# Decoder layer on one core: queries turned one tile further ahead in two attention stages, compression rows turned first, four stores issued one stage later

## What is computed

```python
def compress_kv(rows, cmp_pe, cmp_w1, cmp_b1, cmp_w2, k_norm_cmp):
    ...                                  # blocks of 32 rows, stride 16, flattened
    h = jax.nn.gelu(jnp.einsum('bngcf,cfh->bngch', flat, cmp_w1) + cmp_b1)
    out = jnp.einsum('bngch,chd->bngcd', h, cmp_w2)
    return rmsnorm(out[..., 0, :], k_norm_cmp), out[..., 1, :], end_pos

k_c, v_c, end_c = compress_kv(kv_cmp_p, cmp_pe, cmp_w1, cmp_b1, cmp_w2, k_norm_cmp)
o_cmp_p, p_cmp_p = dense_attend(q_p, k_c, v_c, end_c[None, :] <= pos_p[:, None])
...
def mem_attend(q_raw, kv_mem, mem_q_norm):
    q = rmsnorm(q_raw.reshape(B, S, MEM_H, 1, MEM_HD), mem_q_norm)
    o, _ = dense_attend(q, kv_mem[..., 0, :], kv_mem[..., 1, :], ...)
```

## Time and profile before

| | us |
|---|---|
| median of the timed runs | 2593.41 |
| the profiled execution, its own time | 2588.36 |
| its span, first to last instruction | 2586.8 |
| last copy of the projection ends, to first matmul of the memory stage | 656.49 to 660.17 |
| memory stage, first matmul to last copy | 660.17 to 721.59 |
| turning stage | 721.92 to 754.90 |
| compressed attention | 755.23 to 794.99 |

### The profile page before, as it was taken

How to read it: one execution, slowest core, us unless ns; L and a number is a source line. 1 busy time by engine, 2 the same in 40 slices (tenths; PEclk the granted TensorE clock), 3 DMA queues, 4 the chain that set the end, 5 groups by cost and what they waited for, 6 DMA issues and landing times. The chain is left out here.

```text
span 2586.8 us, 40413 instructions
## 1 busy us (share of the span) xinstructions
PE 2395.7 (93%) x15386; PEld 2183.8 (84%) x15386; DVE 1212.6 (47%) x2152; ACT 817.1 (32%) x1787; POOL 318.3 (12%) x568
## 2 busy tenths in 40 slices
PE   6998897999767999878899999999999999999999
PEld 6977787999666889844499999987999999999997
DVE  4457665314647867556532323333443333333334
ACT  5354463444335665423231212121311111111110
POOL 1004221011103422265200000000000000000000
PEclk9988699999988999989999999999999999999999
DMA  4012432321110000077311112130211111111111
GB/s 150 24 34 65 135 113 82 93 102 30 43 35 1 1 1 2 18 189 185 97 50 38 48 50 82 49 115 1 82 49 33 49 50 49 49 33 50 50 33 66
DMA packets 216764, 156.77 MB, mean 61 GB/s; under 512 B 76722, under 2 KB 197733, under 8 KB 216516
## 3 DMA queue, kind: packets, MB, share of 16 engines
q1 hardware_dynamic: 187124, 122.06, 16.6%
q0 software_dynamic: 8096, 18.98, 2.7%
q10 hardware_dynamic: 21360, 13.22, 1.8%
HBM read 142.76 MB, written 15.59 MB: 61 GB/s over the span
## 5 line engine op out<-in xcount | busy, mean ns | idle before, releaser
L177 PE MATMUL ps<-brT_r,ff_wih 128*128 128x344 f32 x1008 | 322.0, 319 | 0.0
L179 PE MATMUL ps<-brT_r,ff_wi_r 128*128 128x344 f32 x1008 | 321.6, 319 | 0.0
L178 PE MATMUL ps<-xnT_r,ff_wih 128*128 128x344 f32 x1008 | 321.3, 319 | 0.0
L3749 ACT ACTIVATE ff_sa<-ps 128x344 f32<-128x344 f32 x66 | 30.3, 459 | 563.4 <-PE ps L179 563.3
L177 PE MATMUL ps<-x_r,mg_wh 128*128 128x344 f32 x576 | 185.4, 322 | 6.8 <-DVE xnT_r L165 6.8
L177 PEld LDWEIGHTS ps<-brT_r,ff_wih 128*128 128x128 f32 x1008 | 189.6, 188 | 1.0
L179 PEld LDWEIGHTS ps<-brT_r,ff_wi_r 128*128 128x128 f32 x1008 | 189.4, 188 | 0.0
L178 PEld LDWEIGHTS ps<-xnT_r,ff_wih 128*128 128x128 f32 x1008 | 189.0, 187 | 0.4
L178 PE MATMUL ps<-xnT_r,mg_wh 128*128 128x344 f32 x576 | 184.7, 321 | 0.0
L3785 DVE TENSOR_TENSOR x<-x,ps 128x512 f32<-128x512 f32 (+1 forms) x198 | 134.8, 685 | 101.0 <-PE ps L179 100.2
L179 PE MATMUL ps<-x_r,mg_w_r 128*128 128x344 f32 x552 | 176.2, 319 | 0.0
(11 more groups left out here) (615 smaller groups left out, 5879.6 us busy)
## 6 DMA issues: line engine op xcount, KB each, us to landing
ff_wi<-in_w_ffn_in SPq DMA_DIRECT2D x42, 512.0 KB, 5.2
mg_w<-in_w_in SPq DMA_DIRECT2D x23, 512.0 KB, 4.1
ff_wo<-in_w_ffn_out SPq DMA_DIRECT2D x11, 1024.0 KB, 4.9
s_pages<-in_cache_kv_slc POOLq DMA_DIRECT2D x128, 64.0 KB, 2.9
s_pages<-in_cache_kv_slc SPq DMA_DIRECT2D x128, 64.0 KB, 2.8
sc_X<-in_cache_kv_cmp SPq DMA_DIRECT2D x56, 128.0 KB
sc_X<-in_cache_kv_cmp POOLq DMA_DIRECT2D x56, 128.0 KB, 2.4
mg_w<-in_w_branch SPq DMA_DIRECT2D x23, 256.0 KB, 4.5
```

What stands on the lines that cost most here:

```text
L177: nc.tensor.matmul(out, wh, xh, start=(first and k == 0), stop=False)
L178: nc.tensor.matmul(out, wh, xl, start=False, stop=False)
L179: ins = nc.tensor.matmul(out, wl, xh, start=False, stop=(last and k == n - 1))
L3749: nc.scalar.activation(sa[:, s % 2, :], ps[:, s % 2, 0:BLK], ACT.Silu).then_inc(silued, 1)
```

## The change

- In both attention stages, round i now begins with turn(i+3) on PE and with keep_q(i+3) on ACT. Before, these stood behind turn_p(i+1) and keep_p(i+1). The start is reordered to match.
- In the turning stage the x items come first. ACT copies two of them and DVE two. PE waits for w1 alone ahead of the hidden layer. w2 and gcmp are loaded from POOL's queue. Both memsets stand at the start of DVE's stream, and the copies of vc2 stand behind the sum of squares.
- The four stores of the projection stage are issued in the memory stage, behind kv_mem_prompt.

```diff
@@ stage_tok_proj, SP
                 sp.wait_ge(kept, xlast[KV] + 1)
-                sp.dma_start(O["kv_slc_prompt"]..., kvsw[:, 0:QT, 0:256]).then_inc(out, 16)
-                sp.dma_start(O["kv_slc_sample"]..., kvsw[0:B, QT, 0:256]).then_inc(out, 16)
-                sp.dma_start(O["win_prompt"]..., kvsw[:, QT - 4:QT, 256:512]).then_inc(out, 16)
-                sp.dma_start(O["win_sample"][:, WIN - 1]..., kvsw[0:B, QT, 256:512]).then_inc(out, 16)
                 sp.wait_ge(moved, 16)
@@ stage_turn
-        for r in range(4): ... items.append(("k", r, half))
-        for g in range(G): ... items.append(("x", g, half))
+        items = [("x", g, half) for g in range(G) for half in range(2)]
+        NX = len(items)
+        items += [("k", r, half) for r in range(4) for half in range(2)]
@@ stage_turn, SP and POOL
-                sp.dma_start(w2[:, :, :], I["cmp_w2"].rearrange("c h d -> h c d")).then_inc(in_w, 16)
-                sp.dma_start(gcmp[:, :], I["k_norm_cmp"].partition_broadcast(P)).then_inc(in_w, 16)
+                pool.dma_start(w2[:, :, :], I["cmp_w2"].rearrange("c h d -> h c d")).then_inc(in_w2, 16)
+                pool.dma_start(gcmp[:, :], I["k_norm_cmp"].partition_broadcast(P)).then_inc(in_w2, 16)
@@ stage_turn, PE
-                    if n >= 4:
-                        pe.wait_ge(kept, n - 3)
-                        pe.wait_ge(klow, min(n - 3, 8))
+                    if n >= 2 * NX:
+                        pe.wait_ge(klow, n - 2 * NX + 1)
+                    elif n >= NX:
+                        pe.wait_ge(kept_a if n % 2 == 0 else kept_v, (n - NX) // 2 + 1)
...
-                pe.wait_ge(in_w, 64)
-                pe.wait_ge(kept, len(items))
+                pe.wait_ge(in_w, 32)
+                pe.wait_ge(kept_a, NX // 2)
+                pe.wait_ge(kept_v, NX // 2)
...
-                pe.wait_ge(hready, 1)
+                pe.wait_ge(in_w2, 32)
+                pe.wait_ge(klow, 8)
                 pe.wait_ge(activated, 2)
@@ stage_turn, ACT and DVE
+                    elif n % 2 == 0:                     # ACT: x items 0 and 2
+                        for dst, rows in rows_x(n): nc.scalar.activation(dst, rows, ACT.Copy)
+                        if n % 2:                        # DVE: x items 1 and 3
+                            for dst, rows in rows_x(n): nc.vector.tensor_copy(dst, rows)
@@ stage_turn, DVE
+                nc.vector.memset(vc2[:, :, :], 0.0).then_inc(hready, 1)
+                nc.vector.memset(kc2[:, :, :], 0.0).then_inc(hready, 1)
...
-                dve.wait_ge(activated, 2)
-                nc.vector.memset(vc2[:, :, :], 0.0).then_inc(hready, 1)
                 dve.wait_ge(outp, 1)
-                for k in range(2):
-                    nc.vector.tensor_copy(vc2[k * 64:k * 64 + NC, ...], o4[:, 1])
                 ... # ko, its square, the sum, kmean
+                for k in range(2):
+                    nc.vector.tensor_copy(vc2[k * 64:k * 64 + NC, ...], o4[:, 1])
                 dve.wait_ge(kroot, 1)
-                chain.link(dve, nc.vector.memset(kc2[:, :, :], 0.0))
@@ stage_cmp_prompt and stage_mem_prompt, PE (ACT likewise with keep_q, exponentials, keep_p)
                 for i in range(QT):
+                    if i + 3 < QT:
+                        turn(i + 3)
                     if i + 2 < QT:
                         scores(i + 2)
                     if i + 1 < QT:
                         turn_p(i + 1)
-                    if i + 3 < QT:
-                        turn(i + 3)
                     attend(i)
@@ stage_mem_prompt, SP
                 sp.dma_start(O["kv_mem_prompt"]..., kvm[:, :, :]).then_inc(A["prep_out"], 16)
+                ... # the four stores, in the same order
```

More of the change, by code:

```diff
@@ L1582, in stage_turn, with rows_x @@
         klow = sem("klow")
[L1584 to L1590, removed]
+        items = [("x", g, half) for g in range(G) for half in range(2)]
+        NX = len(items)
+        items += [("k", r, half) for r in range(4) for half in range(2)]
+        def rows_x(n):
+            _, r, half = items[n]
+            for cc in range(2):
+                for par in range(2):
+                    yield (xc[par * HD:(par + 1) * HD, cc, r, half * 256:(half + 1) * 256],
+                           ps[cc * HD:(cc + 1) * HD, n % 4, :].rearrange("p (t e) -> p t e", e=2)[:, :, par])
         with st.block() as block:
@@ L1638, in _ @@
                 for n, (kind, r, half) in enumerate(items):
-                    act.wait_ge(turned, n + 1)
                     if kind == "k":
[L1641 to L1649, removed]
+                        act.wait_ge(turned, n + 1)
+                        high(nc, kT[0:HD, r, half * 512:(half + 1) * 512], ps[0:HD, n % 4, :]).then_inc(khigh, 1)
+                    elif n % 2 == 0:
+                        act.wait_ge(turned, n + 1)
+                        for dst, rows in rows_x(n):
+                            ins = nc.scalar.activation(dst, rows, ACT.Copy)
+                        ins.then_inc(kept_a, 1)
                 act.wait_ge(hid, 1)
@@ L1662, in _ @@
             def _(dve):
-                for n, (kind, r, half) in enumerate(items[:8]):
+                nc.vector.memset(vc2[:, :, :], 0.0).then_inc(hready, 1)
+                nc.vector.memset(kc2[:, :, :], 0.0).then_inc(hready, 1)
+                for n, (kind, r, half) in enumerate(items):
+                    if kind == "x":
+                        if n % 2:
+                            dve.wait_ge(turned, n + 1)
+                            for dst, rows in rows_x(n):
+                                ins = nc.vector.tensor_copy(dst, rows)
+                            ins.then_inc(kept_v, 1)
+                        continue
                     cols = slice(half * 512, (half + 1) * 512)
-                    dve.wait_ge(kept, n + 1)
+                    dve.wait_ge(khigh, n - NX + 1)
                     low(nc, kT[HD:P, r, cols], ps[0:HD, n % 4, :], kT[0:HD, r, cols]).then_inc(klow, 1)
-                dve.wait_ge(in_w, 64)
-                dve.wait_ge(activated, 2)
-                nc.vector.memset(vc2[:, :, :], 0.0).then_inc(hready, 1)
-                dve.wait_ge(hready, 1)
+                dve.wait_ge(hready, 2)
+                dve.wait_ge(in_w2, 32)
                 dve.wait_ge(outp, 1)
                 o4 = ps[0:NC, 0, 0:4 * HD].rearrange("p (c g d) -> p c g d", c=2, g=2)
-                for k in range(2):
-                    nc.vector.tensor_copy(vc2[k * 64:k * 64 + NC, :, k * HD:(k + 1) * HD], o4[:, 1])
                 chain.link(dve, nc.vector.tensor_copy(ko[:, :, :], o4[:, 0]))
@@ L1803, in _ @@
                         keep_p(i + 1)
-                    if i + 3 < QT:
-                        keep_q(i + 3)
             @block.vector
@@ L2261, in _ @@
                 exponentials(0)
+                keep_q(2)
                 exponentials(1)
-                keep_q(2)
                 keep_p(0)
                 for i in range(QT):
+                    if i + 3 < QT:
+                        keep_q(i + 3)
                     if i + 2 < QT:
```

28 lines of the change are left out of this document (16 added, 12 removed).

## The result

The changed kernel took 2578.35 us (median of 4 runs, 2569.68 to 2579.30), beside it the kernel before 2594.03 (4 runs, 2590.64 to 2599.18): ratio 0.9928, 95% interval 0.9904 to 0.9952. Between the medians it is 15.7 us less. On another chip it gave 2576.96 against 2589.32 (5 and 16 runs): ratio 0.9948, 0.9930 to 0.9965, or 12.4 us less between the medians. The prediction was 2577.5, a gain of 15.9, which lies inside both intervals.

What follows compares the result with a forecast made beforehand. It took stage barriers and, in both attention stages, a ring through the query copy keep_q as bounds, no engine. Gains of 3.1 + 4.7 + 2.4 + 5.7 = 15.9 us from 2593.41 gave 2577.5, range 2571 to 2585.5.

Steps and rivals of the forecast that it cites:

- Stores: Barrier between projection and memory stage: without SP's four stores there, PE starts 3.15 us earlier; taken as 3.1.
- the cover on SP: Memory stage: SP's moved issues end 3.6 us before its next one, which waits for POOL, so they delay nobody.
- Memory stage: Rounds fall from 6.45 to 5.41 us once scores no longer wait for keep_q; five rounds 5.2, net 4.7.
- The head: Start of the memory stage: turn(3) now stands before scores(2) on PE, costing 0.57 us.
- Turning stage: Hidden layer starts 1.35 us earlier, memset of vc2 off the chain 0.43, vc2 copies 0.58; sum 2.4.
- the move of w2 and gcmp to POOL's queue: Turning stage: these 96 KB beside w1 delay it by 0.4 us at w1's rate, of which 0.3 was taken.
- The other two terms: Turning stage behind the hidden layer: no wait for the vc2 memset, 0.43 us; vc2 copies inside DVE's wait, 0.58.
- Compressed attention: Same ring through keep_q opened: rounds fall from 4.59 to 3.61 us, the head costs 0.2; net 5.7.
- Sum: All four parts together, 3.1 + 4.7 + 2.4 + 5.7 = 15.9 us, giving 2577.5; chance 0.68.
- The rival of more than the sum: PE's bound in the memory stage and a warm hidden layer give 2 to 3 us more, 2574.5; chance 0.05.
- DVE's ring: Memory stage: maximum to end of scaling 4.78 us plus output copy 0.63 bounds the new round at 5.41.
- The rival on the other side, the clock: Later stages: 50 us more at TensorE's 1.2 GHz level make the kernel slower, 2602.5 us; chance 0.04.

Runs made afterwards that it cites:

- e3: Changed kernel with w2 and gcmp loaded from SP's queue behind w1, not from POOL's: 2578.52 us, ratio 0.9966 to the kernel before.
- e5: Changed kernel with POOL issuing the w2 and gcmp loads only once w1 has landed: 2579.94 us, ratio 0.9964 to the kernel before.
- e9: Changed kernel run again unaltered, beside the kernel before on another chip: 2576.96 us, ratio 0.9948.
- e2: Changed kernel with the four stores issued at the end of the projection stage again: 2585.84 us, ratio 0.9982 to the kernel before.
- e10: Changed kernel with w2 and gcmp loaded once w1 has landed and POOL's rotation begun after tile 1's scaling: 2578.89 us, ratio 0.9955 to the kernel before.
- e11: As e10, with DVE's output copy also ahead of the scaling in the memory stage: 2572.64 us, ratio 0.9945 to the kernel before.
- e4: Changed kernel with POOL's rotation of the queries begun only once tile 1 is scaled: 2576.67 us, one run.

## Why the prediction was right, point by point

- **Stores.** Predicted 3.15, measured 3.16, and the cover on SP was 4.3 us for the 3.6 computed. Not foreseen: a shorter gap also keeps PE's clock up, which gave 0.88 in the first transposes and 1.19 at the first maximum. The prediction had read 4.09 us of idling as lost time only, though it had drawn this very inference for the hidden layer.
- **Memory stage.** Predicted 4.7, measured 5.54. The rounds came as worked out, 5.38 against 5.41, worth 5.39. The head was charged 0.57 and gained 0.14. The 1.19 from the clock are in it, and PE took up tile 0's transposes 1.35 earlier in the stage. The chain from there to tile 2's maximum gave 1.21 back, since it ran at the low clock as before (3.94 us of idling, before 4.10) and had turn(3) in it: 0.86 at that clock, charged at 0.57. The two scalings beside POOL, 2.41 and 2.26, were 2.29 and 1.22 before. The first is on this chain, but it was held up before too. The second is not, since DVE then waits 2.82 for the scores. The sum itself was also rounded up: 5.2 - 0.57 is 4.6, not 4.7.
- **Turning stage.** Predicted 2.4, measured 1.27. This is the failed term: the move of w2 and gcmp to POOL's queue was put at 0.3, by bytes, and against e3 and e5 it cost 0.8 and 1.1. The reading under it was wrong too. Before, the small loads stood behind w1 only in the order of issue: w2 was issued at 725.0 and landed at 732.4, the second w1 load at 732.0, so w2 already flew beside w1. What was new is that they were issued from POOL, ahead of the second w1 load. Without them w1 still needed 8.6 to 8.9 from its issue and not 8.3, which is not explained. The second w1 load's issue took 1.38 to 3.76 us beside POOL's issues and 1.21 to 1.57 without, but this is not the cause: in e9 it took 1.50, and w1 landed 10.1 after its issue. The hidden layer started 0.17 earlier, not 1.35. The Trainium skill's section on issuing engines, cited in the prediction, holds in so far as POOL's queue was no path of its own. The other two terms came out at 0.47 (0.10 of it in the hidden layer itself) and 0.63 for 0.43 and 0.58.
- **Compressed attention.** Predicted 5.7, measured 5.30. The rounds are 3.61 but for one of 3.93, in which DVE idled 0.36. The same gap stands in the other profiles with the new order (rounds 3.67 on average), and I have not explained it. The head cost 0.26, predicted 0.2.
- **Sum.** 15.9 predicted, 15.27 in the profiles, 15.7 and 12.4 between medians. Errors of about one microsecond, 0.8 more in the memory stage and 1.1 and 0.4 less in the other two, nearly cancelled. That is luck, and so is part of the absolute time: the base of 2593.41 was the median of three runs, and on the other two chips with many runs the kernel before had 2588.76 and 2589.32. The rival of more than the sum did not come: the hidden layer began at 1.2 GHz (granted clock 0.57), and DVE's ring and not PE bounded the memory stage. The rival on the other side, the clock, did not decide. The prediction's price for it, half of each microsecond, is 2.6 us per 0.001 of mean clock, and the timed runs gave 1.9 to 2.0. e2, e10 and e11 lose 3 to 4 us to it, and it is the likely reason why gains of 1 to 3 us in the stages could not be found again in the medians.

## What to carry to other kernels

Where PE waits each round for a copy on another engine, look at what stands ahead of that copy in its engine's order, and move it ahead of the instruction that closes the ring. Here the new round was then the longest ring through one engine's own order, and could be read off that engine's rows of before. A stage's start and end are worth as much as a round: here a gap of 4 us in which PE idled cost more than 4 us, at the barrier and again ahead of the first turn_p of the memory stage. And small loads that are needed late are better not issued from a second queue ahead of a large one that is needed first: here they did the least harm behind it on its own queue, or once it had landed.

## What the runs showed of the hardware

- PE started the memory stage at 1.2 GHz after idling 4.1 us (first transposes 1.84 to 1.94), and at 2.4 GHz after 0.92 us (1.06). The first scores behind a slow start took 3.68 in e2, where the changed kernel took 1.97. The compressed attention began at 1.2 GHz after only 0.95 us, behind sparse work.
- 96 KB of small loads issued from POOL at the start of 2 MB of w1 on SP: the second w1 load landed 9.4 to 10.5 us after its issue (seven profiles), and 8.6 to 8.9 without them or with them behind w1 on SP (four profiles). By the rate of w1 itself they are worth 0.4.
- Beside POOL's work even DVE instructions on 128x4 elements took 1.01 us (changed kernel) and 1.68 us (e4) for 0.17, and POOL's own last step took 2.42 for 1.39. Each ended as if it had waited for the other's instruction to end: 661.60 against 661.57 for the one of 1.01, 672.59 against 672.57 for the one of 1.68.
